# Rows fetched back by two transfers in flight, a flag that adds them once, and norms by halves, in a YOCO trunk of one core

## The reference

```
layer 0: xn = modulate(rms_norm(h, norm_mix[0]), sh1, sc1);  h += g1 * retention_mixer(xn)
         xn = modulate(rms_norm(h, norm_ffn[0]), sh2, sc2);  h += g2 * grouped_moe(xn)
layer 1: hn = modulate(rms_norm(h, norm_kv), sh_kv, sc_kv)   # shared keys and values from hn
         xn = modulate(rms_norm(h, norm_mix[1]), sh1, sc1);  h += g1 * mla_attention(xn, shared k, v)
         xn = modulate(rms_norm(h, norm_ffn[1]), sh2, sc2);  h += g2 * grouped_moe(xn)
out = rms_norm(h, final_norm)
grouped_moe: 16 experts in 4 groups; scores = sigmoid(xn @ w_router); of the group with the best
  pair of biased scores the two best experts are taken, weighted by their scores;
  expert(x) = (silu(x @ w_gate) * (x @ w_up)) @ w_down, with 512 hidden columns
rms_norm(x, g) = x * rsqrt(mean(x * x) + 1e-6) * g;   modulate(x, sh, sc) = x * (1 + sc) + sh
sh*, sc*, g* = pieces of silu(c) @ w_mod + b_mod, a matrix times one vector
```

## Time and profile before

| | us |
|---|---|
| three executions | 901.22, 904.38, 905.69; median 904.38 |
| the profiled execution, its own time | 903.16 |
| its span in the trace | 901.4 |
| PE busy | 849.8 (94%) |
| DVE, ACT, POOL busy | 326.1, 172.7, 161.1 |
| mean granted TensorE clock | 0.983 |
| retention layer, up to its MoE | about 0 to 298 |
| MoE of layer 0 | about 298 to 524 |
| norm, shared keys and values, attention | about 524 to 642 |
| MoE of layer 1 | about 642 to 893 |
| last norm and store | about 893 to 901 |

### The profile page before, as it was taken

One profiled execution on the slowest core, in us unless ns is written; L12 is line 12 of the kernel. 1 busy time (PEld: TensorE's weight loads), 2 busy tenths in 40 slices (PEclk: granted clock), 3 DMA queues, 4 the chain that ended last, 5 costly groups with the idle time before them and its releaser, 6 DMA issues.

```text
span 901.4 us, 11811 instructions
## 1 busy us (share of the span) xinstructions
PE 849.8 (94%) x4369; PEld 469.9 (52%) x4369; DVE 326.1 (36%) x592; ACT 172.7 (19%) x342; POOL 161.1 (18%) x271
## 2 busy tenths in 40 slices
PE   6999999999999899999999788999799999999994
PEld 3787444444444545545554356864445554554551
DVE  2826765945302212211111158775611112211113
ACT  2100112121102222112211031330322112212111
POOL 0023000000004422112211033200642221111111
PEclk9999999999999899999999899999999999999998
DMA  9989989997479499999999995779699999889994
GB/s 318 387 305 376 375 342 360 341 384 311 189 296 373 193 404 420 421 422 421 421 422 420 341 376 192 282 294 402 241 353 419 419 422 421 354 348 420 422 372 100
DMA packets 70014, 317.29 MB, mean 352 GB/s; under 512 B 10039, under 2 KB 10170, under 8 KB 44366
## 3 DMA queue, kind: packets, MB, share of 16 engines
q1 hardware_dynamic: 61594, 304.42, 84.3%
q0 software_dynamic: 4976, 8.40, 3.8%
q10 hardware_dynamic: 3396, 3.80, 1.4%
HBM read 311.31 MB, written 15.20 MB: 362 GB/s over the span
## 4 chain that ended last, share of the span: by engine, by line
PE 76%; DMA 15%; DVE 4%; ACT 2%; issue 2%; SPq 1%; ACTq 0%; POOL 0%; DVEq 0%; POOLq 0%
PE bank L726 12%; PE bank L908 10%; PE bank L926 10%; PE bank L895 9%; PE bank L767 6%; PE bank L870 5%; DMA h<-outs 5%; PE bank L667 5%; DMA part<-in_moe_w_up 3%; DMA ring<-in_moe_w_up 3%; DMA outs<-arena,row_id 2%; PE bank L1123 2%; PE bank L719 2%; DMA turned<-y 1%; PE bank L1077 1%
## 5 line engine op out<-in xcount | busy, mean ns | idle before, releaser
L1753 DVE TENSOR_TENSOR arena<-bank,arena 128x256 f32<-128x256 f32 x34 | 20.9, 616 | 255.7 <-PE bank L908 255.7
L1506 DVE SCALAR_TENSOR_TENSOR part<-ring,cpad,part 128x1024 f32<-128x1024 f32 x84 | 111.1, 1323 | 3.1 <-DVE part L1506 0.7
L726 PE MATMUL bank<-ring,xnT 128*128 128x512 f32 x256 | 111.2, 592 | 0.0
L895 PE MATMUL bank<-ring,arena 128*64 128x512 f32 x416 | 92.1, 595 | 0.0
L926 PE MATMUL bank<-ring,arena 128*64 128x512 f32 x352 | 81.8, 606 | 2.8 <-issue 2.7
L908 PE MATMUL bank<-ring,arena 128*64 128x256 f32 x704 | 80.3, 381 | 0.8 <-DMA ring<-in_moe_w_up 0.8
L726 PEld LDWEIGHTS bank<-ring,xnT 128*128 128x128 f32 x256 | 48.4, 190 | 59.4 <-issue 59.4
L870 PEld LDWEIGHTS bank<-arena,y 128*128 128x128 f32 x544 | 64.6, 198 | 15.1 <-issue 15.1
L870 PE MATMUL bank<-arena,y 128*128 128x128 f32 x544 | 67.7, 285 | 1.1 <-DVE arena L1714 1.0
L908 PEld LDWEIGHTS bank<-ring,arena 128*64 128x64 f32 x704 | 50.1, 137 | 30.8 <-issue 9.2
L1301 ACT ACTIVATE arena<-bank,modc,scale 128x128 f32<-128x128 f32 x68 | 25.6, 457 | 180.7 <-PE bank L870 180.7
(11 more groups left out here) (330 smaller groups left out, 1069.2 us busy)
## 6 DMA issues: line engine op xcount, KB each, us to landing
ring<-in_w_mod SPq DMA_DIRECT2D x48, 1024.0 KB, 11.7
ring<-in_moe_w_gate SPq DMA_DIRECT2D x48, 1024.0 KB, 17.5
ring<-in_moe_w_down SPq DMA_DIRECT2D x44, 1024.0 KB, 15.8
ring<-in_moe_w_up SPq DMA_DIRECT2D x40, 1024.0 KB, 13.8
ring<-in_ret_w_in SPq DMA_DIRECT2D x24, 1024.0 KB, 8.1
arena<-in_moe_w_down SPq DMA_DIRECT2D x12, 1024.0 KB, 17.3
arena<-in_moe_w_up SPq DMA_DIRECT2D x12, 1024.0 KB, 17.9
arena<-in_moe_w_gate SPq DMA_DIRECT2D x9, 1024.0 KB, 12.4
```

What stands on the lines that cost most here:

```text
L726: ins = pe.matmul(pair[tt][:], xnT[:, k, tok(tt)], w[:, k, :], start=(k == 0), stop=(k == KT - 1))
L895: ins = pe.matmul(bank[0][e * 64:(e + 1) * 64, :], xgT[:, k, e * 64:(e + 1) * 64], w(e, k), start=(k == 0), stop=(k == KT - 1))
L1506: ins = dve.scalar_tensor_tensor(o, w[:, k, :], c, o, ALU.mult, ALU.add)
```

## The change

- The two fetches of `outs[l]` are asked for one behind the other, with no wait between. Rank 0 is still added into `h` by the DMA; rank 1 is a plain copy into the tile `part`. DVE adds it: behind `hidT`'s copy, ahead of the waits for `yg`, a round of the last pair waits for `back_in`, does `h += part * first_time` over 128 x 2048, then sets the one-column flag `first_time` to 0, so that a second round of that pair adds nothing. The flag is set to 1 ahead of the rounds. `h_added` counts 6 a round, for the two steps more.
- The squares behind a MoE layer are taken by halves of columns, each as soon as its part of `into_h` is there (`squares_behind`). The mean of the first half, with epsilon, enters the root as its bias; DVE computes it for both tiles behind `into_h`.
- ACT does a root of a constant (`sqrt_ready`) behind each MoE's rounds and ahead of layer 1's MoE, which puts the table load there.
- `normed_h`: DVE scales tile 0 in two halves, with the reciprocal of tile 1 between; ACT scales tile 1 (`y1_ready`).
- `vectors(3)` and `scales(3)` stand in `mixed(1)` behind `weighted(2)`, not ahead of `ffn_vectors(1)`.
- The semaphores `gains_turned` and `qa_raw` are folded into `rows_turned` and `kr_raw`.

```diff
+        first_time = sb("first_time", [P, 1])
...
@@ PE, turn_y @@
                 for tt in range(TT):
-                    pe.wait_ge(y_ready, 2 * n + tt + 1)
+                    if tt == 0:
+                        pe.wait_ge(y_ready, 2 * n + 1)
+                    else:
+                        pe.wait_ge(y1_ready, 1)
...
@@ ACT @@
+            def sqrt_ready():
+
+                A(stat[:, 20:21], eps[:], ACT.Sqrt)
+
+            def squares_behind(l):
+
+                total = act.value_load(bounds[l][0:1, PAIRS:PAIRS + 1], min_val=PAIRS, max_val=ROUNDS * PAIRS * (l + 1))
+                for i in range(4):
+                    n2, tt = i // 2, i % 2
+                    c = slice(n2 * 512, (n2 + 1) * 512)
+                    act.wait_ge(S["h_added"], total * 6 + i)
+                    A(y[:, tt, c], h[:, tt, c], ACT.Square, accum_out=msq[:, i:i + 1]).then_inc(squares, 1)
+                    if n2:
+                        act.wait_ge(squares, 4 * l + 2 + i + 1)
+                        act.wait_ge(meansq, 2 * l + 2 + tt + 1)
+                        A(root[:, tt:tt + 1], msq[:, i:i + 1], ACT.Sqrt, bias=var[:, tt:tt + 1], scale=1.0 / D).then_inc(roots, 1)
...
             experts(0)
+            sqrt_ready()
...
-            squares_of(2)
+            squares_behind(0)
+            act.wait_ge(rstd1_ready, 1)
+            A(y[:, 1, :].rearrange("p (k j) -> p j k", k=KT), h[:, 1, :].rearrange("p (j k) -> p j k", k=KT), ACT.Copy,
+              scale=rstd[:, 1:2]).then_inc(y1_ready, 1)
...
             copy_rows(3, mla_bank[6])
+            sqrt_ready()
             experts(1)
-            squares_of(4)
+            sqrt_ready()
+            squares_behind(1)
...
@@ DVE, inverse_rms and normed_h @@
+                elif tt == 0:
+                    for i in range(TT):
+                        dve.wait_ge(squares, 2 * n - 2 + i + 1)
+                        dve.tensor_scalar(var[:, i:i + 1], msq[:, i:i + 1], 1.0 / D, EPS, ALU.mult, ALU.add).then_inc(meansq, 1)
...
+            def normed_h():
+
+                own.step(dve, inverse_rms(2, 0))
+                o, a = y[:, 0, :].rearrange("p (k j) -> p j k", k=KT), h[:, 0, :].rearrange("p (j k) -> p j k", k=KT)
+                dve.tensor_scalar(o[:, 0:64], a[:, 0:64], rstd[:, 0:1], None, ALU.mult)
+                inverse_rms(2, 1).then_inc(rstd1_ready, 1)
+                dve.tensor_scalar(o[:, 64:128], a[:, 64:128], rstd[:, 0:1], None, ALU.mult).then_inc(y_ready, 1)
...
@@ DVE, mixed @@
                 for i in range(3):
                     weighted(i)
+                if l:
+                    vectors(3, cols[:, :, 10:12])
+                    scales(3, MOD_COL[1] + 32, gcol[:, :, 3])
...
@@ DVE, experts @@
+                own.step(dve, dve.memset(first_time[:], 1.0))
...
+                    if last:
+                        dve.wait_ge(back_in, 32 * (l + 1))
+                        dve.scalar_tensor_tensor(h[:], part[:], first_time[:], h[:], ALU.mult, ALU.add).then_inc(S["h_added"], 1)
+                        dve.wait_ge(S["h_added"], u * 6 + 4)
+                        dve.memset(first_time[:], 0.0).then_inc(S["h_added"], 1)
                     dve.wait_ge(S["info_ready"], u + 1)
...
                     if last:
-                        dve.wait_ge(back_in, 32 * (l + 1))
                         into_h(u)
...
-            vectors(3, cols[:, :, 10:12])
-            scales(3, MOD_COL[1] + 32, gcol[:, :, 3])
             ffn_vectors(1, mla_bank[2])
...
@@ POOL, experts @@
-                for f in range(2):
-                    pool.dma_start(h[:], outs[l].rearrange("(t p f) n -> f p t n", p=P, f=2)[f], accum_op=ALU.add).then_inc(back_in, 16)
-                    pool.wait_ge(back_in, 32 * l + 16 * (f + 1))
+                back = outs[l].rearrange("(t p f) n -> f p t n", p=P, f=2)
+                pool.dma_start(h[:], back[0], accum_op=ALU.add).then_inc(back_in, 16)
+                pool.dma_start(part[:], back[1]).then_inc(back_in, 16)
+                pool.wait_ge(back_in, 32 * (l + 1))
```

More of the change, by code:

```diff
@@ L325, in build_kernel @@
         dstep = sem("dstep")
-        squares, meansq, roots, y_ready = (sem(n) for n in ("squares", "meansq", "roots", "y_ready"))
+        squares, meansq, roots, y_ready, y1_ready = (sem(n) for n in ("squares", "meansq", "roots", "y_ready", "y1_ready"))
         y_turned, xn_dve, xn_act = sem("y_turned"), sem("xn_dve"), sem("xn_act")
@@ L1396, in inverse_rms, with normed_x @@
                 one = slice(tt, tt + 1)
-                dve.wait_ge(squares, n + tt + 1)
-                dve.tensor_scalar(var[:, one], msq[:, one], 1.0 / D, EPS, ALU.mult, ALU.add).then_inc(meansq, 1)
+                if n == 0:
+                    dve.wait_ge(squares, tt + 1)
+                    dve.tensor_scalar(var[:, one], msq[:, one], 1.0 / D, EPS, ALU.mult, ALU.add).then_inc(meansq, 1)
+                elif tt == 0:
+                    for i in range(TT):
+                        dve.wait_ge(squares, 2 * n - 2 + i + 1)
+                        dve.tensor_scalar(var[:, i:i + 1], msq[:, i:i + 1], 1.0 / D, EPS, ALU.mult, ALU.add).then_inc(meansq, 1)
                 dve.wait_ge(roots, n + tt + 1)
-                own.step(dve, dve.reciprocal(rstd[:, one], root[:, one]))
-            def normed(n):
+                return dve.reciprocal(rstd[:, one], root[:, one])
+            def normed_x():
                 for tt in range(TT):
-                    inverse_rms(n, tt)
-                    o, a = y[:, tt, :], h[:, tt, :]
-                    if n:
-                        o, a = o.rearrange("p (k j) -> p j k", k=KT), a.rearrange("p (j k) -> p j k", k=KT)
-                    dve.tensor_scalar(o, a, rstd[:, tt:tt + 1], None, ALU.mult).then_inc(y_ready, 1)
+                    own.step(dve, inverse_rms(0, tt))
+                    dve.tensor_scalar(y[:, tt, :], h[:, tt, :], rstd[:, tt:tt + 1], None, ALU.mult).then_inc(y_ready, 1)
+            def normed_h():
[4 more added lines that the diff above has]
+                dve.tensor_scalar(o[:, 64:128], a[:, 64:128], rstd[:, 0:1], None, ALU.mult).then_inc(y_ready, 1)
             def modulate(n, dst, which, shift):
@@ L1781, in _ @@
             experts(0)
-            normed(2)
+            normed_h()
             modulate(2, hnT, 4, MOD_COL[2])
@@ L1870, in _ @@
             for tt in range(TT):
-                inverse_rms(4, tt)
+                own.step(dve, inverse_rms(4, tt))
                 dve.scalar_tensor_tensor(acc[:, tt, :], h[:, tt, :], rstd[:, tt:tt + 1], gate[:, 0, :],
```

41 lines of the change are left out of this document (17 added, 24 removed).

## The result

The changed kernel took **890.99 us** (median of 4 runs, 888.99 to 893.40) against 904.17 for the kernel before (4 runs): ratio 0.9862, 95% interval 0.9834 to 0.989. Its profiled execution took 888.99, with a span of 887.2; the one of before had 903.16 and 901.4. So the profiles differ by 14.2 us.

A forecast was written before the change was run, and what follows sets the result against it. PE was taken as the bound (busy 94% of the span, 76% of the chain). Terms 6.4 - 0.4 + 0.2 + 1.1 + 1.0 + 1.5 = 9.8 us took 903.16 to 893.4, placed at 894.0; range 890 to 899.5.

The forecast's parts named there:

- Layer 1's start: Ahead of layer 1's MoE: moving DVE's wait for `turned` ends PE's 3.83 us wait; gain 6.4 us.
- I gave back 0.4 for the stream: Layer 1's rounds: the weight stream might take back part of the earlier start; 0.4 us, bounds 0 and 1.0.
- Layer 1's last round: Second fetch runs beside the first, landing at 883.9, then DVE adds; gain 1.0 us, bounds 2.1 and a loss of 2.7.
- Layer 0's last round: Second fetch lands at 514.4, its addition covered by PE's weights; gain 0.2 us, bounds 0.5 and a loss of 2.
- Less 0.3, since the second fetch now competes with the `down` weights that PE waits for: Layer 0's last round: 0.3 us taken off the gain for the second fetch delaying PE's weights.
- a sign of being wrong: Prediction is wrong if `part<-outs` lands more than 6 us behind `h<-outs`; expected 2 to 3 in layer 1, about 5 in layer 0.
- the bound set for that cover: Layer 0's last round: PE's weights hide the addition unless the second fetch lands later than 516.
- Layer 0's norm: Behind layer 0's `into_h`: half scalings and hidden table load cut 7.5 us to 6.4; gain 1.1 us.
- Layer 1's norm: Behind layer 1's `into_h`: table load and most half squares hidden, 5.4 us becomes 3.9; gain 1.5 us.
- The stream does not hold layer 1: Rival judged: the weight stream holds layer 1's rounds, so the start's 6.0 us are waited for later; 900.0, chance 0.12.
- The fetches without overlap: Rival, both last rounds: second fetch runs only after the first lands, additions delay PE; 905.3, chance 0.05.
- The case in which all lands early: Rival: all lands early and nothing is given back to the stream; 891, chance 0.05.

The follow-up runs named there:

- x6: The kernel before with only vectors(3) and scales(3) of layer 1 moved to wait later; 894.67 us.
- x2: The changed kernel with a wait between the two fetches, so the second, still a plain copy, starts when the first has landed; 898.50 us.
- x10: The changed kernel itself, unedited, timed again in a later batch; 890.47 us, ratio 0.9873 to the kernel before.
- x3: The changed kernel with the fetches as before: both accumulate, one after the other, with no addition by a flag; 893.72 us.
- x5: The changed kernel with DVE's wide addition done a second time, adding zero times the row; 895.67 us.
- x4: The changed kernel without the three roots of a constant that put ACT's table load ahead; 895.79 us.
- x1: The changed kernel with vectors(3) and scales(3) put back ahead of the router's preparation; 899.03 us.
- x9: The changed kernel with both fetches plain, each with its own semaphore, and two wide DVE additions, rank 0's as soon as landed; 886.22 us.
- x8: The kernel before with only the three roots of a constant added that put ACT's table load ahead; 901.79 us.

## Why the prediction came out as it did

It gave 894.0, with 890 to 899.5; measured were 890.99 and 890.47, inside the range and on its fast side. The mechanism of the largest term is right and shown. That the whole sum of the terms, 9.8 us, lies so near the 10.3 of the stretches is in part luck: layer 0's last round was 2.1 us worse than forecast, and the norms (1.0 and 0.6), the start (0.4) and the rounds (0.5) were better by 2.5 together.

- **Layer 1's start, 6.4 us: right**, with 6.8 measured and, less the clock's part, the same from x6. PE went on to the fourth half without a wait, and the eight records took 3.68 us as forecast 3.7. I gave back 0.4 for the stream; nothing was taken.
- **Layer 1's last round, 1.0: right** (1.14), and by the steps given: the landing was forecast 12.6 us behind the first issue (871.30 to 883.9), and the addition began 12.63 us behind it (860.35 to 872.98). The second fetch landed 2.5 us behind the first (issues at 860.35 and 861.19, 10.1 and 11.8 us to landing), as the 2.5 put for it. Alone such a fetch takes 6.0 us from issue to addition and keeps the engines busy for 3.4 (x2), so the 2.5 is right only as what it adds behind a first fetch that is under way; the rest ran beside that one. The addition took 2.35 us; I had 2.55.
- **Layer 0's last round, a gain of 0.2: wrong**, a loss of 1.9 us (2.3 in x10), at and beyond the bound of 2 that I had named. The step that failed is "Less 0.3, since the second fetch now competes with the `down` weights that PE waits for": it was 2.4 us (20.8 to 23.2 behind the mark), against 0.5 won back since DVE's wait of 1.54 is gone. I had computed that the second fetch needs 2.5 us of the engines, and then let only 0.3 of it reach the weights, though in that stretch the engines were full and PE already waited for them. x2 and x3, in which the second fetch starts only when the first has landed, have the last part of `down` at 21.3 and 21.2 us behind the mark again. The landing was wrong too: 8.0 us behind the first fetch's (issues at 490.14 and 490.99, 14.8 and 22.0 us to landing), where the text has about 5 and names more than 6 as a sign of being wrong. That sign came true in layer 0, and the total did not show it. The addition still stayed hidden behind PE's weights, as x5 shows, though the landing was later than the bound set for that cover: the weights had moved back with it.
- **Layer 0's norm, 1.1: the mechanism right, the size short**; 2.1 measured. The term "PE's 1.8 and 1.97 for two tiles" took its durations from rows behind a wait of PE of 2.36 us; behind one of 0.54 they were 1.09 each, 1.6 us less (the granted clock from 530 to 532 was 0.50 in the kernel before), of which PE's wait for the modulated tile, 1.68 us and not 1.26, took back 0.4. Part of x4's loss is the same effect.
- **Layer 1's norm, 1.5**; 2.1 measured. In the row of after, the last scaling ends 3.36 us behind the additions, where I had summed 3.9: root and reciprocal took 0.7 us and the step between the scalings 0.1, for which I had 0.9 and 0.3.
- **POOL's earlier release, nothing**: right; what looked like 1.6 us in x3 was the clock.
- **The rivals.** The stream does not hold layer 1: x6 and x1. The addition is not slow: 2.35 us for 2048 columns, also beside POOL's picks, 1.17 for each 1024 where the earlier trace rows have 1.285; the rule of the Trainium skill (Vector Engine (DVE) Microarchitecture Reference, "Points that are easy to get wrong") of half the throughput, by the prediction's estimate 4.3 us, does not hold for this instruction. The fetches without overlap were real as a price: x2's last rounds are 4.9 and 3.9 us longer than before, where I had 5.4 and 5.3. In the changed kernel they overlapped. The case in which all lands early was put at 891; by the bounds of its terms (1.1, 0.3 and 0.4 better than the forecast's 894.0) it is 892.2.
- The terms gave 9.8 us, the stretches of the profile that the change touches 10.3. Between the profiled executions there are 3.9 us more, from the part up to layer 0's last round, where the changed kernel does the same work but for a few instructions at its start. The medians differ by 13.2, with an interval of some 2.5 us on either side, and do not tell whether any of that belongs to the change.

## What to carry to other kernels

A wait can cost three times: for itself, for the engine whose work is queued behind it, and for PE's clock afterwards; so first move a long wait for a small transfer behind whatever others need, which here was worth more than all other parts together. Where PE already waits for weights with full DMA engines, count another transfer against it in full: the plain 1 MB here moved the last weights back by 2.4 us, and its bytes take 2.5 at the stream's rate. An adding transfer costs more than its bytes: the last weights came as late with one adding fetch ahead of them (the kernel before, 20.7 us) as with two plain ones (x9, 20.7). (The second adding fetch of the kernel before was asked for at 509.37, but the engines still moved 410 GB/s from 509 to 514 and 267 from 514 to 518, so most of its bytes seem to have come behind those weights.) In layer 0, plain transfers into a free buffer, added on an engine that idles, each as soon as it lands, beat it. Judge a small edit by stretches between marks of its profile and by the duration of a fixed group of products, since the clock alone moves the whole by several us.

## What the runs showed of the hardware

- An adding transfer of 1 MB in the last round keeps the engines busy for 6.2 us, a plain one of the same shape for 3.4 (x2, 0.57 of the 6.00 us from 874.2); beside weights the adding one brings the rate down from 411 to 416 GB/s to 308 to 342 at full engines. The software queue's packets took 3.8% of 16 engines' span in the kernel before, 3.1% with one adding transfer a layer, 2.6% with none, for the same 8.40 MB.
- The clock can be lost at work that no edit touched: the same 32 products took 3.81, 5.44, 6.60 and 6.75 us in different kernels, with the granted clock at 1.00 throughout for the first and at 0.50 for part or most of the others. The wait of PE ahead of the turning does not tell which: it was 3.11 us in x4, 2.36 in the kernel before and 0.54 in the changed kernel, which have 3.81, and 2.06 in x8, 1.89 in x6, 1.74 in x3 and 0.54 in x5, which have more. What decides it stays open.
- ACT's copy that writes with a stride took 2.06 us for 1024 columns, against 1.06 for a square of 1024 in order. The two differ in the function too; no run separates it from the stride.
